# Bank order in a two-block transformer kernel: takes one by one, two transposes to other banks, a split last projection

## The reference, cut to what matters

```python
# first model, two layers
x = x + hybrid_mixer(rms_norm(x), w_in, ...)        # 8 neighbourhood heads + 8 grouped heads
x = x + memory_cross_attention(rms_norm(x), ...)    # 4 heads over 256 memory rows
x = x + conv_ffn(rms_norm(x), w_up, ..., w_down)    # 1024 -> 2*2816 -> 1024
x = rms_norm(x)
# second model, two layers
x = x + 0.5 * swiglu(rms_norm(x), ...)              # "f1"
proj = rms_norm(x) @ w_in                           # z, xbc, dt, q, k, v
xbc = silu(causal_conv4(xbc))                       # 16 tiles of 128 features
y = concat(ssd_mixer(xbc, dt, z), dilated_attention(norm(q), norm(k), v))
x = x + y @ w_out
x = x + 0.5 * swiglu(rms_norm(x), ...)              # "f2"
```

## Time and profile before

| | |
|---|---|
| median of the runs | 1901.78 us |
| profiled execution, its own time | 1901.99 us |
| span of that execution in the trace | 1900.2 us |
| PE busy | 99% of the span |
| PE weight loads busy | 86% |
| DVE busy | 77% |
| ACT busy | 62% |
| POOL busy | 21% |
| DMA, share of 16 engines | 53%, 331.96 MB |

### The profile page before, as it was taken

How to read it: one execution, slowest core, us unless ns; L and a number is a source line. 1 busy time by engine, 2 the same in 40 slices (tenths; PEclk the granted TensorE clock), 3 DMA queues, 4 the chain that set the end, 5 groups by cost and what they waited for, 6 DMA issues and landing times.

```text
span 1900.2 us, 29600 instructions
## 1 busy us (share of the span) xinstructions
PE 1890.3 (99%) x11178; PEld 1630.4 (86%) x11178; DVE 1459.9 (77%) x2601; ACT 1173.6 (62%) x2167; POOL 395.6 (21%) x448
## 2 busy tenths in 40 slices
PE   9999999999999999999999999999999999999999
PEld 8889988887898888888987788888888897878887
DVE  7877996587799769866787977856885687897873
ACT  6767775567678556545667565545554667756552
POOL 2210211011011004411022214401440112223430
PEclk9999999999999999999999999999999999999999
DMA  9344666543455656565552355555555544345553
GB/s 367 124 134 144 197 199 225 167 155 117 139 188 190 207 170 201 190 197 178 175 165 93 122 185 192 189 189 187 191 189 192 187 155 151 105 144 179 191 195 124
DMA packets 90973, 331.96 MB, mean 175 GB/s; under 512 B 10064, under 2 KB 10320, under 8 KB 90448
## 3 DMA queue, kind: packets, MB, share of 16 engines
q1 hardware_dynamic: 90832, 330.08, 52.6%
HBM read 328.99 MB, written 1.05 MB: 174 GB/s over the span
## 4 chain that ended last, share of the span: by engine, by line
PE 91%; DVE 4%; ACT 3%; DMA 1%; issue 1%; SPq 0%; ACTq 0%; DVEq 0%
PE PS L83 88%; PE PS L86 3%; DVE WL L98 1%; DVE TMP L108 1%; ACT WH L92 1%; ACT TMP L95 1%; DVE SM L114 1%; DMA RAW<-wts 1%; DMA TMP<-xt 0%; ACT M L92 0%; ACT TMP L92 0%; ACT TMP L94 0%; DVE SM L108 0%; DVE SM L98 0%; DVE TMP L98 0%
## 5 line engine op out<-in xcount | busy, mean ns | idle before, releaser
L98 DVE TENSOR_TENSOR WL<-RAW,WH 128x1024 fp32r<-128x1024 f32 (+1 forms) x610 | 760.5, 1252 | 283.6 <-ACT WH L92 280.3
L92 ACT ACTIVATE WH<-RAW 128x1024 fp32r<-128x1024 f32 (+1 forms) x610 | 640.3, 1053 | 316.6 <-PE PS L83 311.6
L83 PE MATMUL PS<-HX,WH 128*128 128x512 f32 (+1 forms) x1920 | 523.4, 344 | 0.8 <-DVE WL L98 0.4
L83 PE MATMUL PS<-WH,GX 128*128 128x512 f32 (+1 forms) x1632 | 523.4, 392 | 0.0
L83 PE MATMUL PS<-GX,WH 128*128 128x256 f32 (+1 forms) x1776 | 450.9, 331 | 0.9 <-issue 0.5
L83 PE MATMUL PS<-HX,WL 128*128 128x256 f32 x1488 | 413.9, 281 | 0.0
L83 PEld LDWEIGHTS PS<-HX,WH 128*128 128x128 f32 x1920 | 331.0, 189 | 47.3 <-DVE TMP L108 1.1
L83 PEld LDWEIGHTS PS<-WH,GX 128*128 128x128 f32 x1632 | 305.6, 188 | 63.2 <-issue 2.5
L83 PE MATMUL PS<-GX,WL 128*128 128x256 f32 x1264 | 355.7, 281 | 0.0
L83 PEld LDWEIGHTS PS<-GX,WH 128*128 128x128 f32 x1776 | 301.1, 190 | 37.1 <-issue 1.3
L83 PE MATMUL PS<-WL,GX 128*128 128x512 f32 (+1 forms) x816 | 316.6, 388 | 0.0
(11 more groups left out here) (146 smaller groups left out, 1702.0 us busy)
## 6 DMA issues: line engine op xcount, KB each, us to landing
RAW<-wts SPq DMA_DIRECT2D x607, 512.0 KB, 3.7
M<-bias SPq DMA_DIRECT2D x4, 512.0 KB, 12.5
M<-bias SPq DMA_DIRECT2D x1, 2048.0 KB, 10.4
X<-x SPq DMA_DIRECT2D x2, 512.0 KB, 10.6
M<-mem SPq DMA_DIRECT2D x1, 1024.0 KB, 13.3
M<-memt SPq DMA_DIRECT2D x1, 1024.0 KB, 12.2
out<-X SPq DMA_DIRECT2D x4, 256.0 KB, 3.4
CST<-cst SPq DMA_DIRECT2D x1, 794.0 KB, 12.1
```

Of the source, the lines that this page charges most:

```text
L83: return Issued(self.eng and self.eng.matmul(o, l, r, start=first, stop=last, skip_group_check=share))
L92: return Issued(self.eng.activation(o, i, f, scale=scale))
L98: return Issued(self.eng and self.eng.tensor_tensor(o, a, b, op))
```

## The change

Three edits. (1) `fm_four` takes its four banks one at a time, each just ahead of the first matmul of its tile, instead of all four at the start. (2) The two transposes of the queries after steps 1 and 2 of `tm_wide(("v2", L, 0))` go to banks 2 and 3 instead of 7 and 6; the four later ones stay at 7, 6, 7, 6. (3) In the last projection the second column half is written by `last_down`: steps 0 to 19 as before, then the last two steps first for token tile 0, then for tile 1 columns 0 to 255, then for tile 1 columns 256 to 511. The last piece goes to a fresh bank ("rest"), which holds only the contribution of steps 20 and 21. DVE's `last_update` adds tile 0, tile 1 at full width, and then the "rest" bank to the last 256 columns. SP stores five pieces, the last two of 128 KB.

```diff
             def fm_four(keys, acts, st, by, allowed=WHOLE, over=None):
-                ps = [take(k, allowed)[:, 0:S] for k in keys]
+                ps = []
                 HALF[keys[0], 0] = at[0] // 8
                 for part in range(2):
                     for n in range(4):
+                        if part == 0:
+                            ps.append(take(keys[n], allowed)[:, 0:S])
                         if part == 0 and n == (3 if st and st[0] in ("mq", "ffn") else 2) and st is not None:
                             turn_x(st, 1, by, allowed if st[0] == "ffn" else WHOLE)
...
                     if 1 <= i < 7:
-                        turn_qk((0, 2, 3)[(i - 1) // 2], (i - 1) % 2, (7 - (i - 1) % 2,))
+                        turn_qk((0, 2, 3)[(i - 1) // 2], (i - 1) % 2, ((2, 3, 7, 6, 7, 6)[i - 1],))
...
+            def last_down(name, acts):
+                for _ in tm_wide((name, 0), acts, 512):
+                    pass
+                key = (name, 1)
+                for _ in tm_wide(key, acts[:-2], 512, ends=False):
+                    pass
...
+                rest = take((key, "rest"), WHOLE)[:, 0:256]
+                for t, c0, c1, by in ((0, 0, 512, 0), (1, 0, 256, 1), (1, 256, 512, "rest")):
+                    ps = rest if by == "rest" else bank((key, t))[:, c0:c1]
+                    for i in range(2):
...
+                        e.mm(ps, t_cols(ah, t), wh, by == "rest" and i == 0, False)
+                        e.mm(ps, t_cols(ah, t), wl, False, False)
+                        m = e.mm(ps, t_cols(al, t), wh, False, i == 1)
...
+            def last_update(name):
+                key = (name, 1)
+                for t, c0, by in ((0, 0, 0), (1, 0, 1), (1, 256, "rest")):
+                    xs, ps = X[:, t, 512 + c0:1024], bank((key, by))
+                    e.wait_ge(tile, (key, by))
+                    e.wait_ge(xnew)
+                    e.stt(xs, ps[:, 0:512 - c0], 0.5, xs, ALU.mult, ALU.add).then_inc(xnew, (name, 1, by))
...
-            for c in range(2):
-                for t in range(2):
-                    e.wait_ge(xnew, (("f2", DEPTH - 1, "down"), c, t))
-                    e.dma(out[:, t, c * 512:c * 512 + 512], X[:, t, c * 512:c * 512 + 512]).then_inc(stored, (c, t))
-            e.wait_ge(stored, (1, 1))
+            for part, t, c0, c1 in (((0, 0), 0, 0, 512), ((0, 1), 1, 0, 512), ((1, 0), 0, 512, 1024),
+                                    ((1, 1), 1, 512, 768), ((1, "rest"), 1, 768, 1024)):
+                e.wait_ge(xnew, (("f2", DEPTH - 1, "down"), *part))
+                e.dma(out[:, t, c0:c1], X[:, t, c0:c1]).then_inc(stored, part)
+            e.wait_ge(stored, (1, "rest"))
```

More of the change, by code:

```diff
@@ L510, in turn_x, with tm_wide @@
                     m.then_inc(turned, ("xt", st, k // 2))
-            def tm_wide(key, acts, ncol, allowed=WHOLE):
+            def tm_wide(key, acts, ncol, allowed=WHOLE, ends=True):
                 ps = [take((key, t), allowed)[:, 0:ncol] for t in range(2)]
@@ L519, in tm_wide @@
                     wh, wl = WH[:, h % HS, o:o + ncol], WL[:, h % HS, o:o + ncol]
-                    last = i == len(acts) - 1
+                    last = ends and i == len(acts) - 1
                     at[0] += ncol // 128
@@ L647, in rms_over @@
                 put_over(("rb", st), [RX[:, t:t + 1].to_broadcast([128, 128]) for t in range(2)], allowed)
+            def last_down(name, acts):
[4 more added lines that the diff above has]
+                    pass
+                h, o = at[0] // 8, at[0] % 8 * 128
+                assert o == 0
+                at[0] += 8
+                HALF[key, len(acts) - 2] = HALF[key, len(acts) - 1] = HALF[key] = h
+                e.wait_ge(lo, h)
+                rest = take((key, "rest"), WHOLE)[:, 0:256]
+                for t, c0, c1, by in ((0, 0, 512, 0), (1, 0, 256, 1), (1, 256, 512, "rest")):
+                    ps = rest if by == "rest" else bank((key, t))[:, c0:c1]
+                    for i in range(2):
+                        ah, al, made_by = acts[len(acts) - 2 + i]
+                        e.wait_ge(low_of(made_by), made_by)
+                        wh, wl = (w[:, h % HS, 512 * i + c0:512 * i + c1] for w in (WH, WL))
+                        e.mm(ps, t_cols(ah, t), wh, by == "rest" and i == 0, False)
+                        e.mm(ps, t_cols(ah, t), wl, False, False)
+                        m = e.mm(ps, t_cols(al, t), wh, False, i == 1)
+                    m.then_inc(tile, (key, by), *([("half", h)] if by == "rest" else []))
             def residual(name, acts, st=None, allowed=WHOLE, late=None, first=None):
@@ L863, in swiglu @@
                 acts = [(*G(side, m), (f, L, "g", m)) for m in range(FF)]
-                run(residual((f, L, "down"), acts, st))
+                if (f, L) == ("f2", DEPTH - 1):
+                    last_down((f, L, "down"), acts)
+                else:
+                    run(residual((f, L, "down"), acts, st))
             def block2(L):
@@ L2243, in swiglu @@
                         product(p)
-                run(residual((f, L, "down"), FF, *then, scaled=True))
+                run(residual((f, L, "down"), FF, *then, scaled=True, hold=(f, L) == ("f2", DEPTH - 1)))
+                if (f, L) == ("f2", DEPTH - 1):
+                    last_update((f, L, "down"))
             def block2(L):
```

## The result

| | median, us | its kernel before, same chip | ratio, 95% interval |
|---|---|---|---|
| changed kernel | 1913.53 (1912.65 to 1914.15) | 1901.74 | 1.0061 [1.0051, 1.0071] |

The change makes the kernel 11.8 us slower. The forecast was 1910.8 with a range of 1908.6 to 1914.2: sign and range held, the middle was 2.7 us too low. The profiled execution took 1913.27 us by its own time (span 1911.5), 11.28 more than that of the kernel before.

The account below looks back on a forecast made before the run. TensorE (PE), busy 99%, was taken as the bound. 1901.99 + 8.8 (stalls) + 1.2 (clock) - 0.66 (queries) - 0.3 (end) = 1911.0 us, or 1910.8 for the median; range 1908.6 to 1914.2.

Parts of the forecast that it names:

- PE bounds the kernel and passes every stall on: Whole kernel: TensorE is busy 99% of the span, and a delay at the head of an unbroken chain passes whole.
- Bank 2 holds tile 15, released by taps(15) at 987.98: +4.39 per layer: First query transpose after v2 step 1 waits for DVE's last convolution taps; +4.39 us per layer, +8.8 for two.
- at about 1590: Layer 1: expected place of the second 4 to 5 us PE wait on DVE's TMP L108 in the new trace.
- The clock term: PE's clock falling to 1.2 GHz after the two transpose stalls; taken as 1.2 us, between 0 and 4.8.
- half a ramp in all: Sizing of the clock loss over both stalls: 1.2 us, where a full ramp would lose 2.4 us each time.
- a ramp in part or at one stall: The forecast case, clock partly slowed after the two transpose stalls: median 1910.8 us, chance 0.45.
- full ramps at both: Rival: clock falls in full at both transpose stalls, costing 4.8 us, not 1.2; 1914.4 us, chance 0.13.
- The lead of ACT and DVE is used: Rival: small PE stalls after the transposes, 1004 to 1045, close, 0.8 us a layer; 1909.2 us, chance 0.1.
- The queries, -0.66: Layer-1 queries at 353.36: taking fm_four's banks singly removes PE's 0.66 us wait; bounds -0.75 and -0.4.
- The end, -0.3: Split last projection: DVE's updates end 0.17 us sooner, smaller last store saves 0 to 0.4; bounds -0.6 and +0.1.
- Faster if bank 2 were free at 983: Rival: the transposes' old 0.59 us wait goes in both layers with nothing replacing it; 1899.6 us, chance 0.05.

Follow-up runs that it names:

- e7: Changed kernel with the first query transposes in the bank of convolution tile 12 and the second ones in bank 2; 1908.48 us against 1901.76, ratio 1.0034.
- e11: Changed kernel with taps(15) moved earlier in DVE's order, to step 1 before step 2's weight lows; 1908.22 us against 1901.89, ratio 1.0036.
- e2: Kernel before with the second edit alone, query transposes to banks 2 and 3; 1914.99 us against 1902.18, ratio 1.0067.
- e8: e4 with token tile 1 of the last column half stored as one 256 KB piece, not two of 128 KB; 1899.57 us against e4's 1899.41.
- e4: Changed kernel with the two query transposes in the banks of convolution tiles 12 and 13; 1899.84 us against 1902.18 (0.9988), again 1899.41 against 1901.89 (0.9987).
- e10: Changed kernel with 5 unused filler matmuls per layer before the waiting transpose; 1911.12 us against 1901.76, ratio 1.0051.
- e9: Changed kernel with 10 unused filler matmuls per layer before the waiting transpose; 1909.28 us against 1901.76, ratio 1.0039.

## Why the prediction held, and where it was off

- **PE bounds the kernel and passes every stall on.** Right. The shift is flat from one stall to the next, and at 1892 it is what the two places made it.
- **Bank 2 holds tile 15, released by taps(15) at 987.98: +4.39 per layer.** Right: 4.40 and 4.40. e7 and e11 show the releaser, by PE arriving later and by the taps ending sooner. (The second wait was announced "at about 1590"; it ended at 1592.01. The prediction's own 1587.16, moved by the shift of 4.84 that layer 1 came in with, gives 1592.00.)
- **The clock term, taken as 1.2 with bounds 0 and 4.8.** The term that was mis-sized: it measured 3.82 (1.26 and 2.56). I put "half a ramp in all" between two ends, on the argument that a ramp need not be full nor come at both stalls. It came at both, and at 4.8 us idle the clock fell in all four stalls seen (here and in e2). Each cost a little under half of the time at the low level behind the stop, 1.26 for 2.8 us and 2.56 for 5.6 us. The bounds of 0 and 4.8 held for the sum, but 2.4 was not the most for one stall: 2.56 here, 2.73 in e2. By the profiled executions the forecast was 2.27 too low (1911.0 against 1913.27): 2.62 from this term, less 0.08 and 0.22 that the queries and the end gave beyond their terms, less 0.08 of the opening, which adds up to 2.24. So the case that I gave 0.45, a ramp in part or at one stall, is not quite what came; full ramps at both, given 0.13, gave 1914.4 and lay nearer, 0.9 from the result and 0.2 outside my range. That the range held owes something to luck: one of its six runs took 1914.15, against its end of 1914.2. I also wrote that only durations would tell, as the profile's clock reads full in the opening; inside the kernel the granted clock did show both falls. The Trainium skill ("TensorE: Matmul & The Clock Gate", section "HAM oscillation — how this bites in real kernels") says that a TensorE left waiting for data is throttled anew; the traces here agree, with 1.3 to 2.7 us lost at each of the four stops of 4.8 us.
- **The lead of ACT and DVE is used** (a rival, 0.1). Wrong: the four places between 1004 and 1046 where PE's next matmul comes 0.38 to 0.43 us after the one ahead show the same 0.38 to 0.43 in the changed kernel, and ACT waits 3.04 us where it waited 2.58.
- **The queries, -0.66.** Right for the gap, which is 0.66; the matmul behind it gave 0.08 more, so 0.74 in all, just inside the bound of 0.75. No later wait took it back.
- **The end, -0.3.** DVE's 0.17 measured 0.15; the landing was taken at about 0.13, inside its bounds of 0 and 0.4, and measured 0.37. e8 shows that this part is the size of the last store.
- **Faster if bank 2 were free at 983** (0.05, 1899.6 us). The condition did not hold, but its working did: e4 makes it hold, and gives 1899.4 to 1899.8.

Open: what decides whether and for how long the clock falls. At 2.66 to 3.00 us of idle (e10, e11, e7) it fell in five stops of six by the profiled executions, at 4.83 us in four of four, there for about 3.4 us in two and 6.8 in two, with the same work around it. No run tried what the place of a stop in time does by itself.

## What to carry to other kernels

When a tile is moved to another buffer, look up what held that buffer last, and at what time its last reader ends in the trace; do it for the free ones as well, since here two banks of the same set, held by the tiles two and three places older, turned a loss of 11.8 us into a gain of 2.4. If a stop of some microseconds is put on a TensorE that has been at work without a break, add to it what the clock will cost; here 1.3 to 2.7 us for one of 4.8. Filler work for nearly half of the wait did not reliably prevent it, while filling all but half a microsecond did, at no cost, since PE would have stood there anyway. Stretches of 2 us show that fall, a page's slices of 48 us don't.

## What was not expected of the hardware

- The cost of a fall comes in steps. Runs of one and the same kernel fall into two groups, 1910.5 to 1911.1 and 1912.3 to 1912.5 us (e10), or 1907.2 to 1907.6 and 1908.5 to 1909.1 (e7), with a mean clock of 0.999 in the first and 0.998 in the second, while e9, with a full clock, spreads over 0.5 us in five runs.
- A stop of 2.66 us can bring the clock down, and the same stop can leave it (e10).
- The clock can fall when TensorE is already back at work. In layer 1 of e7 the waiting transposes start at 1590.64, yet the clock reads full up to 1592 (stretches of 1 us, columns as before):

```profile
1591.00:1592.00 1.00, 1.00 (x7) 0.86 (x6) 0.96 (x4) 0.67 (x1) 0.00 (x0) 1.00 0.84 262
1592.00:1593.00 1.00, 1.00 (x4) 0.67 (x4) 0.86 (x6) 0.02 (x1) 0.00 (x0) 0.55 0.14 57
```

- A last store of 128 KB released SP 1.95 to 1.97 us after its issue (ten traces), one of 256 KB 2.32 to 2.34 (four traces).
